# Where the weight slots, h and the feed-forward activations lie in SBUF: new bases, and strides of 8204 and 1028 bytes

## The chip, the cores and the metric

The kernel runs on one core of a Trainium2 chip. The metric is device time in microseconds (us). Three timed runs of the kernel before took 2553.0, 2553.1 and 2554.92 us, a median of 2553.1. A difference of 0.2% (about 5 us) is what such runs can tell from no change.

## The reference

Two transformer stacks run one after the other on one sequence of 256 tokens of width 1024, all in float32. The first has two layers, the second four.

```
for l in range(2):                                     # first stack
    h = rms_norm(x, mix_norm_g[l])
    proj = h @ w_in[l]                                 # 1024 x 2660
    mixed = four mixers (moba, mla, stick-breaking, mamba2) on slices of proj
    x = x + mixed @ w_out[l]
    h = rms_norm(x, ffn_norm_g[l])
    u = causal_dwconv(h @ ffn_w_in[l]) + ffn_conv_b[l]  # 1024 x 5632
    x = x + (silu(gate) * up) @ ffn_w_out[l]            # 2816 x 1024
for i in range(4):                                     # second stack
    x = x + 0.5 * rms_norm(swiglu(rms_norm(x), ff1_w_in[i], ff1_w_out[i]))
    x = x + rms_norm(mixer(rms_norm(x)))               # attention a, gated MLP b, attention c, a
    x = x + 0.5 * rms_norm(swiglu(rms_norm(x), ff2_w_in[i], ff2_w_out[i]))
```

The stick-breaking mixer uses a strict causal mask (key before query, the diagonal left out). Nearly all the arithmetic is in the products with the large weights, about 440 MB of them, each used once.

## The kernel before, in words

The five engines each run their own program (classes Sync, Pool, Scalar, Vector and Tensor), written out by hand in one order and tied by semaphores. Nothing is scheduled by a planner: an engine works its list from top to bottom and waits where the list says so.

Weights stream through the chip in chunks of 1 MB, 128 partitions by 2048 words of 4 bytes. SyncE issues one DMA (or a few) per chunk into a slot of `raw`; there are five slots, and a slot is loaded again when the chunk five places before is done. ScalarE rounds the slot into the slot of the same number of `whi` (the high part, type float32r), VectorE subtracts and writes `wlo` (the low part) in place of `raw`, which shares its memory. A product is then three products: high by high, high by low, and low by high. The activations are split in the same way, into the two halves of `h` (eight blocks of 256 words for the high parts, then eight for the low ones) and, for the inner layer of a feed-forward block, into `hid_hi` and `hid_lo` (22 blocks of 256 words each).

TensorE works through these products in four forms, which the profile names by their lines:

- L734, L735, L736 (`tokens_tile`): the stationary operand is 128 words of a block of `h`, the moving operand 256 words of a weight slot.
- L781, L782, L783 (`features_chunk`): the stationary operand is 128 words of a slot, the moving one 256 words of `h`.
- L798, L799, L801 (`wide_chunk`, the inner layer of the second stack): as the last, but L799 moves the high and the low block of `h` in one matmul of 2 x 256 columns.
- L916 (`block`, the products back to width 1024): the stationary operand is 128 words of `hid_hi`, `hid_lo` or `h`, the moving operand 512 words of a slot.

Every one of these operands is read from SBUF at an address that follows from the base of its tensor, the number of its slot (or block) and the stride between slots (or blocks). The bases follow from the order in which `build` makes the tensors: one behind the other.

At the start, SyncE also issues a DMA for the later part of a table of constants (L549), after the fifth chunk of weights. One of these constants, `strict_add`, is only read once, when VectorE copies it and the identity into `masks` in the type float32r (L2504); TensorE adds the mask in the stick-breaking scores. Both VectorE and TensorE (L1114) wait for the table.

Of the kernel before, what the change touches and what calls it, by code (L numbers as in the profile page):

```python
# [26 lines left out]
F32R = mybir.dt.float32r  # L27
I32 = mybir.dt.int32
# [3 lines left out]
P = 128  # L32
SEQ, D, FF = 256, 1024, 2816
TT = SEQ // P
KT = D // P
FT = FF // P
GROUP, HD = 256, 64
# [3 lines left out]
IN = 3 * GROUP + QR + KVR + ROPE + 3 * GROUP + GROUP + XBC + 4  # L41
# [14 lines left out]
BIG = -1e30  # L56
# [5 lines left out]
SLOTS = 5  # L62
AHEAD = 3
CW = 2048
# [7 lines left out]
CONST = {}  # L72


def constants():

    parts, at = [], 0

    def add(name, a):
        nonlocal at  # L80
        a = np.asarray(a, np.float32)
        parts.append(a)
        CONST[name] = (at, at + a.shape[1])
        at += a.shape[1]

    r, c = np.arange(P)[:, None], np.arange(P)[None, :]
    add("ident", r == c)
    add("minus_half", np.full((P, 16), -0.5))
    for name, dim in (("inv64", HD), ("inv32", ROPE)):
        inv = np.float32(1) / (np.float32(THETA) ** (np.arange(0, dim, 2, dtype=np.float32) / np.float32(dim)))  # L90
        add(name, np.broadcast_to(inv.astype(np.float32), (P, dim // 2)))
    add("upto", r <= c)
    add("ones", np.ones((P, P)))
    add("zeros", np.zeros((P, P)))
    add("causal", np.where(c <= r, 0, BIG))
    add("upto_add", np.where(r <= c, 0, BIG))
    add("strict_add", np.where(r < c, 0, BIG))
    add("from_neg", -(r >= c).astype(np.float32))
    add("ones_neg", -np.ones((P, P)))
    add("dist", -np.abs(np.arange(P)[:, None] + np.arange(SEQ)[None, :] - 127))  # L100
    return np.concatenate(parts, 1)


# [12 lines left out]
ROW_TILES = -(-N_ROWS // P)  # L116
# [389 lines left out]
class Sync(Program):  # L506
# [28 lines left out]
    def mix(self, l):  # L535
        e, m, s, d = self.e, self.m, self.s, self.d
        wv = d.w_in[l].rearrange("(k p) c -> p k c", p=P)

        def pick(raw, j):
            to, of, at = [], [], 0  # L540
            for col, n in IN_PIECES[j][1]:
                to.append(raw[:, :].rearrange("p (k c) -> p k c", k=KT)[:, :, at:at + n])
                of.append(wv[:, :, col:col + n])
                at += n
            return to, of
        for b in range(1 if l == 0 else 0, IN_CHUNKS):
            self.chunk(b, 0, pick)
            if l == 0 and b == 4:
                e.dma_start(m.consts[:, CONST["upto"][0]:], d.consts[:, CONST["upto"][0]:CONST["dist"][0]]).then_inc(s.tables_in, 16)  # L549
        self.advance(IN_CHUNKS)  # L550

    def product_tokens(self, what, l, n):
# [64 lines left out]
class Tensor(Program):  # L617
# [452 lines left out]
    def mix(self, l):  # L1070

        e, m, s = self.e, self.m, self.s
        ps, proj, ident = m.ps, m.proj, m.ident
        r = self.round("mixers")
# [14 lines left out]
        for t in range(TT):  # L1089
            e.transpose(ps[:, 2, t * P:(t + 1) * P], m.cn[:, t, 0:P], ident)  # L1090
            e.transpose(ps[0:64, 2, 256 + t * P:256 + (t + 1) * P], m.cn[:, t, P:QR], ident)
            ins = e.transpose(ps[:, 3, t * P:(t + 1) * P], m.cn[:, t, QR:QR + KVR], ident)
# [18 lines left out]
        chunk(5)  # L1111

        if r == 1:
            e.wait_ge(s.tables_in, 16)  # L1114
        e.wait_ge(s.a_ready, r)
        e.wait_ge(s.up_used, 2 * r)
        for t in range(TT):
# [2 lines left out]
        for t in range(TT):  # L1120
            ins = e.matmul(ps[:, 6, t * 4:t * 4 + 4], m.upto, m.a[:, t, :], start=True, stop=True)
# [753 lines left out]
class Vector(Program):  # L1875
# [582 lines left out]
    def mix(self, l):  # L2458
# [40 lines left out]
        self.split(4, 0)  # L2499
        if l == 0:  # L2500
            self.rotary_angles()
            e.wait_ge(s.tables_in, 16)
            for i, name in enumerate(("ident", "strict_add")):
                ins = e.tensor_copy(m.masks[:, i, :], m.cst(name))  # L2504
            ins.then_inc(s.masks_made, 1)
            self.extend_bias()
        self.split(5, 0)
# [496 lines left out]
def build(nc, d):  # L3004
    with ExitStack() as ctx:
        m = Memory()

        def sb(stack, name, shape, dt=F32):
            return stack.enter_context(nc.sbuf_tensor(name, shape, dt))


        m.whi = sb(ctx, "whi", [P, SLOTS, CW], F32R)
        m.zeros = m.whi[:, SLOTS - 1, 0:256]
        m.x = sb(ctx, "x", [P, TT, D])
        m.xn = sb(ctx, "xn", [P, TT, D])
        m.consts = sb(ctx, "consts", [P, CONST["dist"][0]])
        m.cols = sb(ctx, "cols", [P, ROW_TILES * P])
        m.masks = sb(ctx, "masks", [P, 2, P], F32R)
        m.trig = sb(ctx, "trig", [P, 192])
        m.ss = sb(ctx, "ss", [P, 2])  # L3020
        m.ms = sb(ctx, "ms", [P, 2])
        m.rs = sb(ctx, "rs", [P, 2])
        m.ss2 = sb(ctx, "ss2", [P, 2, 4])
        m.ss3 = sb(ctx, "ss3", [P, 2])
        m.ms2 = sb(ctx, "ms2", [P, 2])
        m.rs2 = sb(ctx, "rs2", [P, 2])
        m.st = sb(ctx, "st", [P, 60])
        m.lam_d = sb(ctx, "lam_d", [P, 4])
        m.ahead = m.lam_d
        m.pos = sb(ctx, "pos", [P, 2])  # L3030
        m.pos_i = sb(ctx, "pos_i", [P, 2], I32)
        m.negmax = sb(ctx, "negmax", [P, 4, 2, 2])
        m.sums = sb(ctx, "sums", [P, 4, 2, 2])
        m.rsum = sb(ctx, "rsum", [P, 4, 6])

        def shared(name, *layouts):

            size, made = 0, []
            for layout in layouts:
                with ExitStack() as inner:  # L3040
                    used = 0
                    for args in layout:
                        made.append(sb(inner, *args))
                        used += int(np.prod(args[1][1:])) * 4
                    size = max(size, used)
            sb(ctx, name, [P, size // 4])
            return made

        (m.rb, m.dt, m.a, m.neg) = shared(
            "mem_scales",  # L3050
            [("rb", [P, SEQ])],
            [("dt", [P, 8, 8]), ("a", [P, TT, 4]), ("neg", [P, 12])])
        (m.raw, m.wlo) = shared(
            "mem_weights",
            [("raw", [P, SLOTS, CW])],
            [("wlo", [P, SLOTS, CW], F32R)])
        m.h = sb(ctx, "h", [P, 2, KT, SEQ], F32R)
        m.h_hi, m.h_lo = m.h[:, 0, :, :], m.h[:, 1, :, :]
        (m.hid_hi, m.hid_lo, m.proj, m.z0, m.z1, m.z2, m.xh, m.xdt, m.bias, m.v, m.qk, m.b_w, m.b_rows, m.b_uv, m.b_wt) = shared(
            "mem_hidden",  # L3060
            [("hid_hi", [P, FT, SEQ], F32R), ("hid_lo", [P, FT, SEQ], F32R)],
            [("proj", [P, TT, IN]), ("z0", [P, 4, 3 * P]), ("z1", [P, 4, 3 * P]), ("z2", [P, 4, 3 * P]), ("xh", [P, TT, GROUP]), ("xdt", [P, TT, GROUP])],
            [("bias", [P, 16, SEQ]), ("v", [P, TT, D]), ("qk", [P, 16, SEQ])],
            [("b_w", [P, 8, P]), ("b_rows", [P, 2, D]), ("b_uv", [P, TT, 2 * D]), ("b_wt", [P, 8, P])])
        (m.u, m.silu, m.hid, m.junk, m.diag, m.prob, m.prob_t, m.prob4, m.rope_tmp, m.moba_x, m.rows) = shared(
            "mem_small",
            [("u", [P, RING, 2, SEQ]), ("silu", [P, RING, SEQ]), ("hid", [P, RING, SEQ])],
# [34 lines left out]
        z1 = m.z1[:, :, :].rearrange("p h c -> p (h c)")  # L3102
        m.ang0, m.turns, m.ang = (z1[:, i * 192:(i + 1) * 192] for i in range(3))
        m.ext = z1[0:32, 576:576 + 3 * P]
        m.y = m.xc[:, 0:2, :]
        m.zs = m.xc[:, 2:4, :]
        m.head_sqs = [m.z1[:, :, :].rearrange("p h c -> p (h c)")[:, i * 512:(i + 1) * 512].rearrange("p (t c) -> p t c", t=TT) for i in range(3)]
# [86 lines left out]
```

## Time and profile before

| | us |
|---|---|
| median of three timed runs | 2553.1 |
| the profiled execution, timed | 2554.75 |
| the span of its instructions | 2552.9 |
| TensorE matmul busy | 2534.4 |
| TensorE weight load busy | 2257.4 |
| VectorE busy | 1770.3 |
| ScalarE busy | 1400.6 |
| GpSimd busy | 156.1 |

The profiled execution took 1.85 us more than its span, and 1.65 us more than the median of the timed runs. A matmul's recorded duration includes its way through the array, so neighbours overlap: a row with a mean of 390 ns does not stand for 390 ns of the span. What a matmul costs in a stream is the distance from its start to the start of the next. It is read from starts in the timeline, or from a count of matmuls in a stretch in which the engine never idles.

### The profile page before, as it was taken

Reading aid. Unit: us, or ns where it says so; the run is one execution under the profiler, and the core shown is the slowest. Engines: PE = TensorE matmul, PEld = TensorE weight load, DVE = VectorE, ACT = ScalarE, POOL = GpSimd, SP = SyncE. Lnnn points to the kernel's source line nnn. Section 1 sums busy time; section 2 is a strip of 40 time slices with the busy share of each in tenths; the row PEclk is TensorE's granted clock in tenths of the full one; section 3 lists DMA queues with packets and bytes.
Section 4 is the critical chain, followed back from the end, with each engine's and each line's share of the span. In section 5 each row is a group of like instructions: output and inputs, shape, how many; then the busy total and the mean of one; then the engine's idle time right before and its main releaser. Section 6 shows DMA issues by size and latency. Waiting matters only on the chain.

```text
span 2552.9 us, 38595 instructions
## 1 busy us (share of the span) xinstructions
PE 2534.4 (99%) x15929; PEld 2257.4 (88%) x15929; DVE 1770.3 (69%) x2517; ACT 1400.6 (55%) x2098; POOL 156.1 (6%) x228
## 2 busy tenths in 40 slices
PE   9999999999999999999999999999999999999998
PEld 8999899998888988888888888888988888898987
DVE  6778567785775677757756775775777567566773
ACT  7756477654554555545555554554655455455652
POOL 2100011000000000000010000002010000010000
PEclk9999999999999999999999999999999999999999
DMA  7267543665765547667665766755467567563863
GB/s 226 94 171 213 179 150 98 176 188 182 192 196 198 190 139 201 196 179 194 197 211 151 205 186 180 202 187 188 155 167 204 185 179 205 185 204 122 217 195 118
DMA packets 568297, 459.96 MB, mean 180 GB/s; under 512 B 10298, under 2 KB 529290, under 8 KB 568122
## 3 DMA queue, kind: packets, MB, share of 16 engines
q1 hardware_dynamic: 562615, 441.91, 58.5%
q0 software_dynamic: 4656, 15.30, 1.7%
q8 instruction: 126, 2.06, 0.3%
q10 hardware_dynamic: 851, 0.28, 0.0%
q14 instruction: 49, 0.40, 0.0%
HBM read 456.37 MB, written 1.10 MB: 179 GB/s over the span
## 4 chain that ended last, share of the span: by engine, by line
PE 94%; DVE 3%; ACT 1%; DMA 1%; issue 0%; POOL 0%; SPq 0%; DVEq 0%; POOLq 0%; ACTq 0%
PE ps L916 28%; PE ps L799 23%; PE ps L798 10%; PE ps L781 5%; PE ps L783 5%; PE ps L782 5%; PE ps L734 4%; PE ps L736 4%; PE ps L735 4%; PE ps L801 1%; PE ps L657 1%; DVE wlo L1890 1%; DMA raw<-in_w_in 1%; PE ps L1017 1%; PE ps L1003 0%; DVE xc L2549 0%
## 5 line engine op out<-in xcount | busy, mean ns | idle before, releaser
L1890 DVE TENSOR_TENSOR wlo<-raw,whi 128x2048 fp32r<-128x2048 f32 (+1 forms) x419 | 956.6, 2286 | 391.0 <-ACT whi L1314 390.8
L1314 ACT ACTIVATE whi<-raw 128x2048 fp32r<-128x2048 f32 (+2 forms) x421 | 800.6, 1907 | 338.1 <-DMA raw<-in_ff_w_out 169.0
L799 PE MATMUL ps<-h,whi 128*128 128x512 f32 x2560 | 865.1, 390 | 0.0
L798 PE MATMUL ps<-h,wlo 128*128 128x256 f32 x2240 | 627.5, 280 | 0.0
L799 PEld LDWEIGHTS ps<-h,whi 128*128 128x128 f32 x2560 | 460.4, 188 | 76.7
L798 PEld LDWEIGHTS ps<-h,wlo 128*128 128x128 f32 x2240 | 420.5, 188 | 13.8
L1314 ACT ACTIVATE u<-ps 128x512 f32<-128x512 f32 x160 | 95.7, 598 | 374.0 <-PE ps L799 373.8
L916 PE MATMUL ps<-whi,hid_lo 128*128 128x512 f32 x880 | 296.1, 396 | 0.0
L916 PE MATMUL ps<-whi,hid_hi 128*128 128x512 f32 x880 | 295.0, 394 | 0.0
L916 PE MATMUL ps<-wlo,hid_hi 128*128 128x512 f32 x880 | 294.4, 394 | 0.0
L781 PE MATMUL ps<-h,whi 128*128 128x256 f32 x1024 | 288.1, 281 | 0.0
L734 PE MATMUL ps<-whi,h 128*128 128x256 f32 (+2 forms) x992 | 283.3, 286 | 3.8 <-ACT proj L1314 2.0
L783 PE MATMUL ps<-h,wlo 128*128 128x256 f32 x1024 | 286.4, 280 | 0.0
L782 PE MATMUL ps<-h,whi 128*128 128x256 f32 x1024 | 286.0, 279 | 0.0
L736 PE MATMUL ps<-whi,h 128*128 128x256 f32 (+2 forms) x992 | 278.4, 281 | 0.0
L735 PE MATMUL ps<-wlo,h 128*128 128x256 f32 (+2 forms) x992 | 278.4, 281 | 0.0
L916 PEld LDWEIGHTS ps<-whi,hid_hi 128*128 128x128 f32 x880 | 165.9, 189 | 38.0
L916 PEld LDWEIGHTS ps<-whi,hid_lo 128*128 128x128 f32 x880 | 165.2, 188 | 38.9
L2251 DVE TENSOR_TENSOR u<-ps,u 128x512 f32<-128x512 f32 x160 | 110.6, 691 | 127.6 <-ACT u L1314 127.3
L916 PEld LDWEIGHTS ps<-wlo,hid_hi 128*128 128x128 f32 x880 | 165.1, 188 | 38.2
L734 PEld LDWEIGHTS ps<-whi,h 128*128 128x128 f32 x992 | 189.0, 191 | 7.8 <-issue 5.0
L781 PEld LDWEIGHTS ps<-h,whi 128*128 128x128 f32 x1024 | 192.6, 188 | 3.0 <-issue 3.0
(321 smaller groups left out, 3203.5 us busy)
## 6 DMA issues: line engine op xcount, KB each, us to landing
raw<-in_ff_w_in SPq DMA_DIRECT2D x176, 1024.0 KB, 6.1
raw<-in_ff_w_out SPq DMA_DIRECT2D x88, 1024.0 KB, 4.9
raw<-in_ffn_w_in SPq DMA_DIRECT2D x44, 1024.0 KB, 6.1
raw<-in_a_w_qkv SPq DMA_DIRECT2D x24, 1024.0 KB, 5.2
raw<-in_ffn_w_out SPq DMA_DIRECT2D x22, 1024.0 KB, 4.9
raw<-in_w_in SPq DMA_DIRECT2D x18, 1024.0 KB, 6.2
raw<-in_c_w_qkv SPq DMA_DIRECT2D x12, 1024.0 KB, 5.3
raw<-in_w_out SPq DMA_DIRECT2D x8, 1024.0 KB, 5.0
```

The costliest lines, as they stand in the source:

```text
L734: e.matmul(out, hi, w_hi, start=(k == 0), stop=False)
L735: e.matmul(out, hi, w_lo, start=False, stop=False)
L736: self.last = e.matmul(out, lo, w_hi, start=False, stop=(k == KT - 1))
L781: e.matmul(out, hi, m.h_hi[:, k, :], start=(k == 0), stop=False)
L782: e.matmul(out, hi, m.h_lo[:, k, :], start=False, stop=False)
L783: ins = e.matmul(out, lo, m.h_hi[:, k, :], start=False, stop=(k == KT - 1))
L798: e.matmul(out[:, 0:SEQ], lo, m.h[:, 0, k, :], start=False, stop=False, skip_group_check=True)
L799: ins = e.matmul(view(out, a=2), hi, m.h[:, :, k, :], start=(k == 0), stop=(k == KT - 1), skip_group_check=True)
L916: self.last = e.matmul(m.ps[:, base + 2 * t + h, :], x, w[:, k, h * 512:(h + 1) * 512], start=(first and k == 0 and n == 0), stop=(last an ...
L1314: return self.nc.scalar.activation(*a, **k)
L1890: self.e.tensor_tensor(chunk_view(m.wlo[:, slot, :], c), chunk_view(m.raw[:, slot, :], c), chunk_view(m.whi[:, slot, :], c).bitcast(F32), ...
L2251: e.tensor_tensor(u, bank[:, :, 0:SEQ], u, ALU.add).then_inc(s.dve_step, 1)
```

## The change

The tensors are made in another order, and three of them get a gap behind each block.

- `masks`, `trig`, `negmax` and `sums` (together 1920 bytes a partition) are made first, so `whi` starts at byte 18432. Behind it come `x`, `xn`, `raw` with `wlo`, `h` and the shared memory of the activations. The small tensors and the constants come after these.
- Slots of `whi`, `raw` and `wlo` are 2051 words long, and 2048 are used: 8204 bytes from slot to slot.
- Blocks of `h`, `hid_hi` and `hid_lo` are 257 words long, and 256 are used: 1028 bytes from block to block.
- To make room, `strict_add` moves to the end of the table of constants and is no longer kept in `consts`. It is loaded by a DMA of its own into `m.strict`, 512 bytes of `z2` (a tensor of the mixers), and read from there once. The two waits for the table count both DMAs.

The starts per partition, as the two programs are built:

| operand | start before | stride before | start now | stride now |
|---|---|---|---|---|
| `whi`, slot | 16512 | 8192 | 18432 | 8204 |
| `raw`, `wlo`, slot | 84896 | 8192 | 75840 | 8204 |
| `h`, block | 125856 | 1024 | 116864 | 1028 |
| `hid_hi`, block | 142240 | 1024 | 133312 | 1028 |
| `hid_lo`, block | 164768 | 1024 | 155936 | 1028 |

Before, each of these starts is a multiple of 32 bytes. Now slot s starts 12 s bytes, and block k starts 4 k bytes, behind a multiple of 16: slots 1, 2 and 3 and three blocks of four are off a multiple of 16 bytes, the others are on one.

```diff
-    add("strict_add", np.where(r < c, 0, BIG))
     add("from_neg", -(r >= c).astype(np.float32))
     add("ones_neg", -np.ones((P, P)))
     add("dist", -np.abs(np.arange(P)[:, None] + np.arange(SEQ)[None, :] - 127))
+    add("strict_add", np.where(r < c, 0, BIG))
...
                 e.dma_start(m.consts[:, CONST["upto"][0]:], d.consts[:, CONST["upto"][0]:CONST["dist"][0]]).then_inc(s.tables_in, 16)
+                e.dma_start(m.strict, d.consts[:, CONST["strict_add"][0]:CONST["strict_add"][1]]).then_inc(s.tables_in, 16)
...
-            e.wait_ge(s.tables_in, 16)
+            e.wait_ge(s.tables_in, 32)
...
-            for i, name in enumerate(("ident", "strict_add")):
-                ins = e.tensor_copy(m.masks[:, i, :], m.cst(name))
+            for i, mask in enumerate((m.ident, m.strict)):
+                ins = e.tensor_copy(m.masks[:, i, :], mask)
...
-        m.whi = sb(ctx, "whi", [P, SLOTS, CW], F32R)
+        m.masks = sb(ctx, "masks", [P, 2, P], F32R)
+        m.trig = sb(ctx, "trig", [P, 192])
+        m.negmax = sb(ctx, "negmax", [P, 4, 2, 2])
+        m.sums = sb(ctx, "sums", [P, 4, 2, 2])
+        m.whi = sb(ctx, "whi", [P, SLOTS, CW + 3], F32R)[:, :, 0:CW]
...
+            [("raw", [P, SLOTS, CW + 3])],
+            [("wlo", [P, SLOTS, CW + 3], F32R)])
+        m.raw, m.wlo = m.raw[:, :, 0:CW], m.wlo[:, :, 0:CW]
+        m.h = sb(ctx, "h", [P, 2, KT, SEQ + 1], F32R)[:, :, :, 0:SEQ]
...
+            [("hid_hi", [P, FT, SEQ + 1], F32R), ("hid_lo", [P, FT, SEQ + 1], F32R)],
...
+        m.hid_hi, m.hid_lo = m.hid_hi[:, :, 0:SEQ], m.hid_lo[:, :, 0:SEQ]
...
+        m.strict = m.z2[:, 0, 0:P]
```

No matmul is added, removed or moved, and none changes its shape. Two places show an instruction more. The first is SyncE's list at the start of the program (`raw` are the slots, `consts` the kept table, `z` the tensor that holds the strict mask for its one use), before:

```order
9 L371 DMA rows<-in_b_b_s 8x128
10 L525 DMA raw<-in_w_in 128x8x224
11 L525 DMA raw<-in_w_in 128x8x4
12 L525 DMA raw<-in_w_in 128x8x256 x3
13 L549 DMA consts<-in_consts 128x1024
14 L525 DMA raw<-in_w_in 128x8x256 x6
15 L525 DMA raw<-in_w_out 128x2x1024 x4
```

and now:

```order
9 L371 DMA rows<-in_b_b_s 8x128
10 L525 DMA raw<-in_w_in 128x8x224
11 L525 DMA raw<-in_w_in 128x8x4
12 L525 DMA raw<-in_w_in 128x8x256 x3
13 L549 DMA consts<-in_consts 128x896
14 L550 DMA z<-in_consts 128x128
15 L525 DMA raw<-in_w_in 128x8x256 x6
16 L525 DMA raw<-in_w_out 128x2x1024 x4
```

The table's DMA has lost 128 of its 1024 columns, and a DMA with these 128 stands behind it, ahead of the sixth chunk of weights. The second place is VectorE's list in the first layer's mixers, before:

```order
35 L1941 TENSOR_SCALAR z<-z 128x192
36 L2504 CAST masks<-consts 128x128 x2
37 L1901 TENSOR_SCALAR z<-consts,z 32x127
38 L1890 TENSOR_TENSOR wlo<-raw,whi 128x2048
39 L2510 TENSOR_REDUCE st<-rope_tmp 128x16
```

and now:

```order
35 L1942 TENSOR_SCALAR z<-z 128x192
36 L2505 CAST masks<-consts 128x128
37 L2505 CAST masks<-z 128x128
38 L1902 TENSOR_SCALAR z<-consts,z 32x127
39 L1891 TENSOR_TENSOR wlo<-raw,whi 128x2048
40 L2511 TENSOR_REDUCE st<-rope_tmp 128x16
```

The two copies stand where they stood; the second reads `z`. Where a copy or a sum writes two neighbouring blocks of `h` at once, its shape is now 128x2x256 in place of 128x512.

## Rows read from the trace of the kernel before

**Rows 1.** The page: busy us (share of the span) x instructions of each engine.

```profile
PE 2534.4 (99%) x15929; PEld 2257.4 (88%) x15929; DVE 1770.3 (69%) x2517; ACT 1400.6 (55%) x2098; POOL 156.1 (6%) x228
```

**Rows 2.** The page: chain that ended last, share of the span by engine, by line.

```profile
PE 94%; DVE 3%; ACT 1%; DMA 1%; issue 0%; POOL 0%; SPq 0%; DVEq 0%; POOLq 0%; ACTq 0%
PE ps L916 28%; PE ps L799 23%; PE ps L798 10%; PE ps L781 5%; PE ps L783 5%; PE ps L782 5%; PE ps L734 4%; PE ps L736 4%; PE ps L735 4%; PE ps L801 1%; PE ps L657 1%; DVE wlo L1890 1%; DMA raw<-in_w_in 1%; PE ps L1017 1%; PE ps L1003 0%; DVE xc L2549 0%
```

**Rows 3.** Waits of TensorE, longest in total: us, times, longest.

```profile
PE ps L734 <- ACT proj L1314: 2.0, 1, 2.0
PE ps L1249 <- DVE z L2634: 1.8, 2, 0.9
...
PE ps L734 <- DVE wlo L1890: 0.6, 1, 0.6
```

**Rows 4.** Groups by line: shapes xcount | busy us, mean ns | idle before.

```profile
L799 PE MATMUL ps<-h,whi 128*128 128x512 f32 x2560 | 865.1, 390 | 0.0
L798 PE MATMUL ps<-h,wlo 128*128 128x256 f32 x2240 | 627.5, 280 | 0.0
L916 PE MATMUL ps<-whi,hid_lo 128*128 128x512 f32 x880 | 296.1, 396 | 0.0
L916 PE MATMUL ps<-whi,hid_hi 128*128 128x512 f32 x880 | 295.0, 394 | 0.0
L916 PE MATMUL ps<-wlo,hid_hi 128*128 128x512 f32 x880 | 294.4, 394 | 0.0
...
L736 PE MATMUL ps<-whi,h 128*128 128x256 f32 x928 | 260.8, 281 | 0.0
L735 PE MATMUL ps<-wlo,h 128*128 128x256 f32 x928 | 260.8, 281 | 0.0
```

**Rows 5.** Timeline of TensorE: start us, us, instruction; a stretch of the wide form.

```profile
1030.02 0.28 PE L798 MATMUL ps<-h,wlo 128*128 128x256 f32 x1
1030.14 0.39 PE L799 MATMUL ps<-h,whi 128*128 128x512 f32 x1
1030.37 0.28 PE L798 MATMUL ps<-h,wlo 128*128 128x256 f32 x1
...
1031.40 0.28 PE L798 MATMUL ps<-h,wlo 128*128 128x256 f32 x1
```

**Rows 6.** Windows: stretch and length, busy (count) by engine, PEclk, DMA share, GB/s.

```profile
1080.00:1120.00 40.00, 40.00 (x174) 32.40 (x173) 16.74 (x8) 13.87 (x10) 0.00 (x0) 1.00 0.58 184
165.00:255.00 90.00, 90.00 (x771) 90.00 (x770) 78.45 (x122) 57.37 (x84) 6.46 (x12) 1.00 0.73 202
10.00:40.00 30.00, 27.31 (x222) 26.73 (x223) 20.41 (x36) 22.66 (x34) 10.84 (x19) 0.96 1.06 327
1130.00:1175.00 45.00, 45.00 (x297) 41.04 (x296) 33.83 (x45) 27.38 (x39) 3.26 (x6) 1.00 0.84 219
```

**Rows 7.** VectorE lines that read at shifting word offsets: ns min/median/max, first and last start.

```profile
L2547 DVE TENSOR_SCALAR xc<-xt,cols x8: 403/404/408, 68.6 to 386.1; 128x256 f32<-128x256 f32 x8
L2549 DVE SCALAR_TENSOR_TENSOR xc<-xt,cols,xc x24: 475/479/489, 70.0 to 391.2; 128x256 f32<-128x256 f32 x24
```

**Rows 8.** The chain's pieces at the start of the program: start us, us, what.

```profile
22.48 0.13 PE ps L736
22.62 11.15 DMA raw<-in_w_in
33.80 1.91 ACT whi L1314
```

**Rows 9.** Timeline of SyncE at the start: start us, us, instruction, count.

```profile
13.15 2.92 SPq L549 DMA_DIRECT2D consts<-in_consts  x1
16.11 39.90 SPq L525 DMA_DIRECT2D raw<-in_w_in  x6
```

**Rows 10.** VectorE's copies into the masks: ns min/median/max, first and last start us.

```profile
L2504 DVE CAST masks<-consts x2: 220/220/221, 46.5 to 46.6; 128x128 fp32r<-128x128 f32 x2
```

More of the change, by code:

```diff
@@ L2501, in mix @@
             self.rotary_angles()
-            e.wait_ge(s.tables_in, 16)
-            for i, name in enumerate(("ident", "strict_add")):
-                ins = e.tensor_copy(m.masks[:, i, :], m.cst(name))
+            e.wait_ge(s.tables_in, 32)
+            for i, mask in enumerate((m.ident, m.strict)):
+                ins = e.tensor_copy(m.masks[:, i, :], mask)
             ins.then_inc(s.masks_made, 1)
@@ L3015, in build, with shared @@
         m.xn = sb(ctx, "xn", [P, TT, D])
+        def shared(name, *layouts):
+            size, made = 0, []
+            for layout in layouts:
+                with ExitStack() as inner:
+                    used = 0
+                    for args in layout:
+                        made.append(sb(inner, *args))
+                        used += int(np.prod(args[1][1:])) * 4
+                    size = max(size, used)
+            sb(ctx, name, [P, size // 4])
+            return made
+        (m.raw, m.wlo) = shared(
+            "mem_weights",
+            [("raw", [P, SLOTS, CW + 3])],
+            [("wlo", [P, SLOTS, CW + 3], F32R)])
+        m.raw, m.wlo = m.raw[:, :, 0:CW], m.wlo[:, :, 0:CW]
+        m.h = sb(ctx, "h", [P, 2, KT, SEQ + 1], F32R)[:, :, :, 0:SEQ]
+        m.h_hi, m.h_lo = m.h[:, 0, :, :], m.h[:, 1, :, :]
+        (m.hid_hi, m.hid_lo, m.proj, m.z0, m.z1, m.z2, m.xh, m.xdt, m.bias, m.v, m.qk, m.b_w, m.b_rows, m.b_uv, m.b_wt) = shared(
+            "mem_hidden",
+            [("hid_hi", [P, FT, SEQ + 1], F32R), ("hid_lo", [P, FT, SEQ + 1], F32R)],
+            [("proj", [P, TT, IN]), ("z0", [P, 4, 3 * P]), ("z1", [P, 4, 3 * P]), ("z2", [P, 4, 3 * P]), ("xh", [P, TT, GROUP]), ("xdt", [P, TT, GROUP])],
+            [("bias", [P, 16, SEQ]), ("v", [P, TT, D]), ("qk", [P, 16, SEQ])],
+            [("b_w", [P, 8, P]), ("b_rows", [P, 2, D]), ("b_uv", [P, TT, 2 * D]), ("b_wt", [P, 8, P])])
         m.consts = sb(ctx, "consts", [P, CONST["dist"][0]])
         m.cols = sb(ctx, "cols", [P, ROW_TILES * P])
-        m.masks = sb(ctx, "masks", [P, 2, P], F32R)
-        m.trig = sb(ctx, "trig", [P, 192])
         m.ss = sb(ctx, "ss", [P, 2])
@@ L3031, in build @@
         m.pos_i = sb(ctx, "pos_i", [P, 2], I32)
-        m.negmax = sb(ctx, "negmax", [P, 4, 2, 2])
-        m.sums = sb(ctx, "sums", [P, 4, 2, 2])
         m.rsum = sb(ctx, "rsum", [P, 4, 6])
[L3036 to L3047, printed above, removed]
         (m.rb, m.dt, m.a, m.neg) = shared(
@@ L3052, in build @@
             [("dt", [P, 8, 8]), ("a", [P, TT, 4]), ("neg", [P, 12])])
[L3053 to L3064, printed above, removed]
+        m.hid_hi, m.hid_lo = m.hid_hi[:, :, 0:SEQ], m.hid_lo[:, :, 0:SEQ]
         (m.u, m.silu, m.hid, m.junk, m.diag, m.prob, m.prob_t, m.prob4, m.rope_tmp, m.moba_x, m.rows) = shared(
```

## The prediction

> **What bounds the kernel now.** I read the busy times first, then the chain, TensorE's waits, the matmul groups, and last windows and a timeline for the cost of one matmul. TensorE's matmuls are busy for 2534.4 of 2552.9 us [rows 1], and the chain of work that ended last runs over TensorE for 94% of the span, nearly all of it in the four forms of the big products [rows 2]. So TensorE waits for almost nothing: 2552.9 - 2534.4 leaves 18.5 us, and its longest single wait is 2.0 us [rows 3]. VectorE at 69% and ScalarE at 55% [rows 1] stand on the chain with 4% together [rows 2], at the edges between stages.
>
> A change of layout can therefore show in three places: in what one matmul costs, in the edges, and in the transfers, if they grow until TensorE waits for them.
>
> What one matmul costs is read from starts. In the wide form an L798 starts at 1030.02 and again at 1030.37 and, four rounds after the first, at 1031.40 [rows 5]: 1.38 us for four rounds, 345 ns for a 256-column matmul and a 512-column one, about 117 and 228. In the products back, 174 matmuls of 512 columns fill 40 us [rows 6]: about 231 ns each. In the first stack's inner layer 771 of 256 columns fill 90 us [rows 6]: 116.7 ns. The clock is granted in full there, at its upper level of 2.4 GHz, so a column a cycle would be 213.3 and 106.7 ns. Each matmul pays 10 to 18 ns more than its columns.
>
> **The change part by part.**
>
> *The operands' addresses.* None of some 14,400 big matmuls (about 5,800 of 512 columns and 8,600 of 256 or a little fewer) goes away or changes its shape. One nanosecond on each would be 14 us, so the answer hangs on a fraction of a nanosecond. Does a matmul's cost follow its operands' addresses? In L735 the moving operand starts at an odd multiple of 32 bytes (`wlo`, 84896), in L736 at an even one (`whi`, 16512), and both have a mean of 281 ns. In L916 the three kinds of product have 394, 394 and 396 ns, and the two with 394 differ in the slot's base, while the 396 has the same moving operand as one of them [rows 4]. So a move by 32 bytes costs 0 to 2 ns and shows no sign. Moves by a word do not occur on TensorE before: every start is a multiple of 32. The nearest rows for those are VectorE's. The taps of the convolution read `xt`, whose rows are 1036 bytes apart, at one, two and three words' offset. The 8 and 24 instructions lie within 403 to 408 and 475 to 489 ns [rows 7], 1% and 3% from end to end for all offsets.
>
> The bounds. Below: were the whole excess over a column a cycle a matter of addresses, and were it to go, 5,800 x 16 + 8,600 x 10 = 179 us would go with it. Above: I take it that a stream is read in groups of words, four to a group; a stream that starts off a multiple of 16 bytes then reads one group more. From 256 to 512 columns the mean goes from 280 to 394 ns [rows 4], 0.445 ns a column, so four columns are 1.8 ns. By the table of starts, 11,700 moving streams are off such a multiple (an L799 has two streams): 21 us. The weight load next to the 256-column matmuls is on the same footing; in 165 to 255 us it is busy all the time [rows 6], so it may pace them, and 5,700 of these loads start off a multiple: 10 us more. I take 0, since the rows nearest, L735 against L736 and VectorE's taps, show no cost of a start; the ends are -179 and +31.
>
> The Trainium skill, "SBUF — State Buffer", section "Specifications (TRN2)", speaks against the change: SBUF has lines of 16 bytes, an access needs at least two hits in a line for full bandwidth, and each crossing to a new line pays a penalty. A stream that starts or ends with a single word in a line would pay by that rule; VectorE's taps above pay at most a few ns, and no row here shows TensorE at such a start. By the rule the sum would go up, by the bound above; by the rows it stays.
>
> *The writers.* ScalarE, VectorE and the edges write `h`, `hid` and the slots at the new starts, and the pairs of blocks as 2x256. By the taps [rows 7] that is 0. Were each of VectorE's and ScalarE's instructions on the chain 1% longer, 4% of 2552.9 is 102 us, so +1 us is the end above. Away from the edges the cover is their idle time, 31% and 45% of the span [rows 1].
>
> *The slots' transfers.* A packet now lands at a start that is no multiple of 32 bytes; no row shows what that costs. The cover is large: in the products back the share of the DMA engines is 0.58, in the first stack's inner layer 0.73, in the densest stretch that I show 0.84, with TensorE never idle [rows 6]. Packets could take 1/0.73 = 1.37 times as long before the inner layer waits. I take 0 there. In 10 to 40 us there is no cover: the share is 1.06 [rows 6], and the chain runs through one transfer that begins when a slot comes free at 22.62 us and lands at 33.80, 11.15 us on [rows 8]. A packet 3% longer is 0.3 us there.
>
> *The mask's own DMA.* It carries bytes that the table's DMA no longer carries, and stands ahead of the six DMAs that SyncE issues from 16.11 us [rows 9]. The first of them for which the chain waits is held until 22.62 us by a slot, not by SyncE, so an issue of under half a microsecond before it has room. Its small packets go through a full queue: up to 0.2 us on the chain. The copies that wait for it start at 46.5 us [rows 10], more than 30 us after the table's issue at 13.15, while a transfer in that full queue takes 11 us [rows 8, 9]. Behind VectorE's wait stand the next `wlo` and the mixers, behind TensorE's the sums; neither waits longer. 0.
>
> *Sum.* The profiled execution took 2554.75 us, span 2552.9 and 1.85 around it. To it come 0.3 + 0.2 = 0.5 at the start and 0 elsewhere: 2555.25. The median of the timed runs stands 1.65 below that execution: 2553.6 us, +0.02%. About 0.2%, 5 us, is what a measurement of this kernel can tell from no change.
>
> **The rivals.**
>
> *Slower by the groups (0.31).* Every stream that starts off a multiple of 16 bytes reads a group more, in TensorE. For it: the cost per column shows no slack in which a fetch could hide, since a 512-column matmul costs 0.445 ns for each added column and not 0.417. Against it: VectorE's taps, and L735 beside L736. The rule of lines on the page "SBUF — State Buffer" of the Trainium skill would have this outcome. It begins to count from 0.4 ns a stream (11,700 x 0.4 = 5 us). Its price is 21 us, 2574.6; with the weight loads 2585.
>
> *Slower by far (0.06).* A word-aligned start is served at a lower rate throughout, by TensorE or by the DMA engines. Were packets to take twice as long, the share of 0.73 in 165 to 255 us [rows 6] would become 1.46, so these 90 us would become 131; with the second layer's that is 82 us, 2636 before the second stack is counted. Nothing in the rows speaks for it but that they can't exclude it.
>
> *Faster by a gentler meeting of the streams (0.23).* The excess of 10 to 18 ns comes from the moving stream and the weight load meeting in SBUF at starts that agree in their low bits, and shifted starts undo a part of it. For it: the excess is there in every form and I have no other cause. Against it: it is the same for both bases [rows 4], and the starts of the two streams drift against each other anyhow. The Trainium skill, "TensorE: Matmul & The Clock Gate", section "Step-by-step: what each phase is for", says that TensorE has two independent read ports, one for each of the streams; no run here shows the ports. A tenth of the 179 us is 18: 2536; a quarter is 45: 2509.
>
> *It doesn't do what it says.* The starts in the table are of the built program, so this is left out.
>
> **How the numbers follow.** No change 0.40, at 2553.6, from 2549 to 2558. Slower by the groups 0.31, some of it (0.03) too small to be told from no change. Slower by far 0.06. Faster 0.23, likewise with 0.02 too small. So faster 0.21, within 0.2% 0.45, slower 0.34. The range reaches over the groups' price with the weight loads, 2590, and to the tenth of the excess, 2535; the quarter and the far case are left out, under 2 in 10. The likeliest case's own range is 2549 to 2558.
>
> **What would show it.** Right: L799, L798 and L916 keep their means of 390, 280 and 394 to 396 ns within 1 ns; TensorE's waits stay those of [rows 3]; the share of the transfers in 165 to 255 us stays near 0.73. Slower by the groups: means 1 to 4 ns up, most in L799, whose two streams both start off, and least in L801, whose block 0 starts on a multiple. Slower by far: TensorE waits for `wlo`, with a DMA behind it, or means up by tens of ns. Faster: means down in all forms. What would make the forecast wrong is a cost or a gain of 0.4 ns a matmul, which no row before can show.

## The result, and the profile after

The changed kernel took 2582.3 us, the median of four runs (2582.17 to 2582.45), against 2553.23 us for the kernel before: a ratio of 1.0112, 95% interval 1.010 to 1.0125. That is 29 us slower, where the likeliest case said no change (2553.6) and the rival "slower by the groups" said 2574.6, or 2585 with the weight loads. Behind the changed lines the line numbers are one higher: L799 is now L800, L916 is L917.

First the page of the changed kernel, busy time by engine (us, share of the span, instructions):

```profile
span 2580.4 us, 38596 instructions
PE 2562.4 (99%) x15929; PEld 2273.2 (88%) x15929; DVE 1771.7 (69%) x2517; ACT 1399.9 (54%) x2098; POOL 158.1 (6%) x228
```

Against [rows 1], matmuls are busy for 28.0 us more, and the span is 27.5 us longer. VectorE, ScalarE and GpSimd moved by 1 to 2 us. The loss is TensorE's own work, then, and no wait. The waits of TensorE say the same (us, times, longest):

```profile
PE ps L1250 <- DVE z L2635: 1.6, 2, 0.8
...
PE ps L735 <- ACT proj L1315: 0.8, 1, 0.8
```

The longest wait of [rows 3], 2.0 us for `proj`, is down to 0.8, and none has come in its place. The groups of matmuls tell where the time went (shapes xcount | busy us, mean ns | idle before):

```profile
L800 PE MATMUL ps<-h,whi 128*128 128x512 f32 x2560 | 883.1, 397 | 0.0
L799 PE MATMUL ps<-h,wlo 128*128 128x256 f32 x2240 | 629.6, 281 | 0.0
L917 PE MATMUL ps<-whi,hid_hi 128*128 128x512 f32 x880 | 296.3, 396 | 0.0
L917 PE MATMUL ps<-whi,hid_lo 128*128 128x512 f32 x880 | 295.3, 394 | 0.0
L917 PE MATMUL ps<-wlo,hid_hi 128*128 128x512 f32 x880 | 295.0, 394 | 0.0
L782 PE MATMUL ps<-h,whi 128*128 128x256 f32 x1024 | 290.5, 284 | 0.0
L783 PE MATMUL ps<-h,whi 128*128 128x256 f32 x1024 | 288.6, 282 | 0.0
L784 PE MATMUL ps<-h,wlo 128*128 128x256 f32 x1024 | 288.1, 281 | 0.0
...
L737 PE MATMUL ps<-whi,h 128*128 128x256 f32 x928 | 261.9, 282 | 0.0
L736 PE MATMUL ps<-wlo,h 128*128 128x256 f32 x928 | 261.7, 282 | 0.0
```

and the same three lines of the first stack's inner layer in the kernel before, which [rows 4] doesn't hold:

```profile
L781 PE MATMUL ps<-h,whi 128*128 128x256 f32 x1024 | 288.1, 281 | 0.0
L783 PE MATMUL ps<-h,wlo 128*128 128x256 f32 x1024 | 286.4, 280 | 0.0
L782 PE MATMUL ps<-h,whi 128*128 128x256 f32 x1024 | 286.0, 279 | 0.0
```

By busy time, L800 lost 883.1 - 865.1 = 18.0 us, L799 2.1, the three of the first stack's inner layer 6.7, the three products of L917 with `hid` only 1.1, and L736 with L737 2.0. That is 29.9 us. At the start 1.4 us come back (below); the rest is in small groups. Counted from start to start, as a matmul's cost is, the sums are much the same: the wide form (L799, L800 and L802) lost 18.9 us, the first stack's inner layer 5.9, L735 to L737 3.2, L917 on `hid` 1.0. Against the kernel before, then, the 512-column matmul that moves two blocks of `h` carries 60% of the loss, and the equally wide one of L917, whose slots moved in the same way, carries next to none. Against the same bases without gaps it looks otherwise (first experiment).

The stretches that the prediction spoke of (length, busy and count by engine, granted clock, DMA share, GB/s):

```profile
1080.00:1120.00 40.00, 40.00 (x174) 32.37 (x173) 19.45 (x11) 16.25 (x11) 0.00 (x0) 1.00 0.55 188
165.00:255.00 90.00, 90.00 (x758) 90.00 (x757) 76.74 (x118) 57.00 (x82) 6.49 (x12) 1.00 0.73 199
10.00:40.00 30.00, 28.59 (x242) 28.08 (x242) 20.39 (x36) 22.56 (x33) 12.97 (x19) 1.00 1.04 326
```

Against [rows 6], the products back make 174 matmuls in 40 us as before, the inner layer 758 in 90 us and not 771 (118.7 ns each, where it was 116.7), and the transfers' share there is still 0.73. The start is not slower: the share is 1.04, and the granted clock is 1.00 where it was 0.96. The chain there (start us, us, what):

```profile
22.04 0.12 PE ps L737
22.18 10.21 DMA raw<-in_w_in
32.41 1.92 ACT whi L1315
```

The transfer starts 0.4 us earlier than in [rows 8] and takes 0.9 us less, so ScalarE begins 1.4 us earlier. In this execution neither the starts of the slots nor the mask's own DMA shows as a cost.

### The profile page after: what moved, and what is told of

Same layout as the page of the kernel before. It is cut to its first block, busy times and chain, and to the rows that moved or that the text cites. A ratio compares the mean times of both kernels' runs of the same rounds, so it can differ in the third digit from the quotient of the medians.

```text
span 2580.4 us, 38596 instructions
## 1 busy us (share of the span) xinstructions
PE 2562.4 (99%) x15929; PEld 2273.2 (88%) x15929; DVE 1771.7 (69%) x2517; ACT 1399.9 (54%) x2098; POOL 158.1 (6%) x228
## 3 DMA queue, kind: packets, MB, share of 16 engines
q1 hardware_dynamic: 562759, 441.91, 58.1%
## 4 chain that ended last, share of the span: by engine, by line
PE 94%; DVE 3%; ACT 1%; DMA 1%; issue 0%; POOL 0%; SPq 0%; DVEq 0%; POOLq 0%; ACTq 0%
PE ps L917 27%; PE ps L800 23%; PE ps L799 10%; PE ps L782 5%; PE ps L783 5%; PE ps L784 5%; PE ps L735 4%; PE ps L736 4%; PE ps L737 4%; PE ps L802 1%; PE ps L658 1%; DVE wlo L1891 1%; DMA raw<-in_w_in 1%; PE ps L1018 0%; PE ps L1004 0%; DVE xc L2550 0%
## 5 line engine op out<-in xcount | busy, mean ns | idle before, releaser
L800 PE MATMUL ps<-h,whi 128*128 128x512 f32 x2560 | 883.1, 397 | 0.0
L799 PE MATMUL ps<-h,wlo 128*128 128x256 f32 x2240 | 629.6, 281 | 0.0
L800 PEld LDWEIGHTS ps<-h,whi 128*128 128x128 f32 x2560 | 460.8, 188 | 89.6
L799 PEld LDWEIGHTS ps<-h,wlo 128*128 128x128 f32 x2240 | 423.5, 189 | 13.6
L917 PE MATMUL ps<-whi,hid_hi 128*128 128x512 f32 x880 | 296.3, 396 | 0.0
L917 PE MATMUL ps<-whi,hid_lo 128*128 128x512 f32 x880 | 295.3, 394 | 0.0
L917 PE MATMUL ps<-wlo,hid_hi 128*128 128x512 f32 x880 | 295.0, 394 | 0.0
L735 PE MATMUL ps<-whi,h 128*128 128x256 f32 (+2 forms) x992 | 283.5, 286 | 2.4 <-DVE h L1953 1.0
L737 PE MATMUL ps<-whi,h 128*128 128x256 f32 (+2 forms) x992 | 279.4, 282 | 0.0
L736 PE MATMUL ps<-wlo,h 128*128 128x256 f32 (+2 forms) x992 | 279.3, 282 | 0.0
L917 PEld LDWEIGHTS ps<-whi,hid_lo 128*128 128x128 f32 x880 | 165.9, 189 | 38.5
L917 PEld LDWEIGHTS ps<-wlo,hid_hi 128*128 128x128 f32 x880 | 165.9, 189 | 38.4
L917 PEld LDWEIGHTS ps<-whi,hid_hi 128*128 128x128 f32 x880 | 165.8, 189 | 37.9
L782 PEld LDWEIGHTS ps<-h,whi 128*128 128x128 f32 x1024 | 193.5, 189 | 3.0 <-issue 3.0
L783 PEld LDWEIGHTS ps<-h,whi 128*128 128x128 f32 x1024 | 194.1, 190 | 0.0
```

The costliest lines, as they stand in the source:

```text
L735: e.matmul(out, hi, w_hi, start=(k == 0), stop=False)
L736: e.matmul(out, hi, w_lo, start=False, stop=False)
L737: self.last = e.matmul(out, lo, w_hi, start=False, stop=(k == KT - 1))
L782: e.matmul(out, hi, m.h_hi[:, k, :], start=(k == 0), stop=False)
L783: e.matmul(out, hi, m.h_lo[:, k, :], start=False, stop=False)
L799: e.matmul(out[:, 0:SEQ], lo, m.h[:, 0, k, :], start=False, stop=False, skip_group_check=True)
```

## The experiments

All times are medians, and ratios are to the kernel before on the same chip with a 95% interval. The runs were on several chips, where the kernel before had medians of 2553.2 to 2553.4 us. "Offset" below is an operand's start within 64 bytes. In the kernel before, `whi` has offset 0, and `wlo`, `h` and `hid` have 32, in every slot and block.

### New bases without gaps

```diff
-        m.whi = sb(ctx, "whi", [P, SLOTS, CW + 3], F32R)[:, :, 0:CW]
+        m.whi = sb(ctx, "whi", [P, SLOTS, CW], F32R)[:, :, 0:CW]
-        m.h = sb(ctx, "h", [P, 2, KT, SEQ + 1], F32R)[:, :, :, 0:SEQ]
+        m.h = sb(ctx, "h", [P, 2, KT, SEQ], F32R)
```

(the same for `raw`, `wlo`, `hid_hi`, `hid_lo`; the order of the tensors and the mask's DMA stay changed; every base is now a multiple of 2048 bytes, and every block of `h` and `hid` starts on a multiple of 1024.)

> The new order of the tensors and the mask's own DMA, with slots 8192 and blocks 1024 bytes apart, so every operand starts on a multiple of 32 bytes again, and whi, h and hid on a multiple of 2048. Theory A (a moving stream that starts off a multiple of 16 bytes costs): as before, 2553 within 3 us, L800 back at a mean of 390 ns. Rival B (it is the new bases or their distances, not the odd starts): it keeps most of the 29 us, above 2570. Rival C (round bases are better and the gaps take more than 29 us back): under 2545.

2556.8 us, 1.0014 (1.0006 to 1.0023): most of the loss hangs on the gaps. But the bases are not free. The groups, as above:

```profile
L800 PE MATMUL ps<-h,whi 128*128 128x512 f32 x2560 | 876.1, 396 | 0.0
L799 PE MATMUL ps<-h,wlo 128*128 128x256 f32 x2240 | 624.6, 279 | 0.0
...
L917 PE MATMUL ps<-whi,hid_hi 128*128 128x512 f32 x880 | 291.3, 390 | 0.0
L917 PE MATMUL ps<-whi,hid_lo 128*128 128x512 f32 x880 | 290.5, 389 | 0.0
L917 PE MATMUL ps<-wlo,hid_hi 128*128 128x512 f32 x880 | 290.5, 389 | 0.0
```

L800's busy time rose by 11.0 us against [rows 4] (6 ns in its mean), and the three products with `hid` fell by 4 to 7 (-13.2 us in all). From start to start, the first stack's inner layer takes 8.2 us more as well. Effects of starts that are all multiples of 32 cancel almost to nothing.

This kernel differs from the changed one by the gaps alone. Against it, from start to start, the changed kernel loses 15.0 us in L917 on `hid` and 3.9 on `h`, 9.4 in the wide form, and wins back 2.3 in the first stack's inner layer. Which form seems to pay depends on the layout that one compares with.

### Gaps in h alone

```diff
-        m.h = sb(ctx, "h", [P, 2, KT, SEQ], F32R)
+        m.h = sb(ctx, "h", [P, 2, KT, SEQ + 1], F32R)[:, :, :, 0:SEQ]
```

(from the kernel without gaps; `hid_hi` and `hid_lo` keep blocks of 1024 bytes.)

> As round_only, and the blocks of h 1028 bytes apart, slots and hid without gaps. Theory A: nearly all of the loss, since L800 (means up by 7 ns on 2560 matmuls, 18 us) and L782 to L784 (up 2 ns on 3072, 5 us) move h: 2574 to 2579, and L917 and L735 to L737 as in round_only. A rival that puts the cost on the weight slots (odd writes and packets, or odd stationary operands in L800): under 2560.

2580.0 us, 1.0101 (1.0085 to 1.0116): 23 us over the kernel without gaps, from `h` alone.

```profile
L800 PE MATMUL ps<-h,whi 128*128 128x512 f32 x2560 | 882.8, 397 | 0.0
...
L917 PE MATMUL ps<-whi,hid_hi 128*128 128x512 f32 x880 | 296.7, 396 | 0.0
L917 PE MATMUL ps<-wlo,hid_hi 128*128 128x512 f32 x880 | 296.0, 395 | 0.0
L917 PE MATMUL ps<-whi,hid_lo 128*128 128x512 f32 x880 | 295.9, 395 | 0.0
```

L917 on `hid` lost 16 us, though within 64 bytes all its operands stand at the same offsets as in the kernel without gaps. The timelines of the two show it. First the kernel without gaps (start us, us, instruction, two to a row; two rows are left out in each):

```profile
1080.40 0.62 PE L917 MATMUL ps<-whi,hid_hi 128*128 128x512 f32 x2
...
1081.76 0.62 PE L917 MATMUL ps<-whi,hid_hi 128*128 128x512 f32 x2
```

and then the one with gaps in `h`:

```profile
1079.69 0.63 PE L917 MATMUL ps<-whi,hid_hi 128*128 128x512 f32 x2
...
1081.09 0.63 PE L917 MATMUL ps<-whi,hid_hi 128*128 128x512 f32 x2
```

Six matmuls take 1.36 us in the one (227 ns each) and 1.40 in the other (233). Both run at that pace, without a wait, through the whole of each such stage. At the granted clock, 1.00 of 2.4 GHz, that is 544 and 560 cycles for 512 columns.

Two things differ for L917 here. The stage before it has other operands, and behind the longer `h` the tensors of `hid` stand 64 bytes further from the slots. No run moves `hid` by 64 bytes against the slots and leaves the stage before as it was, so these 6 ns can't be put down to one of the two. That the offsets alone don't set a pace shows within the kernel before. Near the end of the products back its L916 takes the same products in the same order in all ten of its stages on `hid`, and the stage of the first layer and the second one of the second stack begin with the same slot too, so every operand stands at the same address. Behind the first layer's inner layer it looks so:

```profile
313.67 0.40 PE L916 MATMUL ps<-wlo,hid_hi 128*128 128x512 f32 x1
...
325.58 0.39 PE L916 MATMUL ps<-wlo,hid_hi 128*128 128x512 f32 x1
```

and in that stage of the second stack so:

```profile
1113.24 0.39 PE L916 MATMUL ps<-wlo,hid_hi 128*128 128x512 f32 x1
...
1125.03 0.39 PE L916 MATMUL ps<-wlo,hid_hi 128*128 128x512 f32 x1
```

From the first row to the last are 51 matmuls, in 11.91 us (233.5 ns each) and in 11.79 (231.2). Both stages of the first stack end at the one pace and all eight of the second at the other. So a stream can settle in more than one pace on the same operands. What is seen to differ here is the form of the inner layer before it.

### Gaps in the slots alone

```diff
-        m.whi = sb(ctx, "whi", [P, SLOTS, CW], F32R)[:, :, 0:CW]
+        m.whi = sb(ctx, "whi", [P, SLOTS, CW + 3], F32R)[:, :, 0:CW]
```

(from the kernel without gaps; `raw` and `wlo` likewise.)

> As round_only, and the slots of whi, raw and wlo 8204 bytes apart, h and hid without gaps. Theory A: the matmuls that move a slot alone pay, L735 to L737 1 to 2 ns and L917 0 to 1: 2555 to 2560; L800 at 390 although its stationary operand starts off a multiple of 16 bytes in three slots of five. The rival that puts the cost on the slots: above 2570.

2567.78 us, 1.0057 (1.0045 to 1.007). L800 is at 394 ns, L917 at 395 to 396. With the gaps in `h` (+23) this +11 would make 34; the changed kernel, with both and those of `hid`, has +25.5. The costs don't add. L917 on `hid` is slow again, and here too `hid` stands elsewhere against the slots: 128 bytes further from `whi`, 64 from `wlo`.

### Gaps of 16 bytes

```diff
-        m.whi = sb(ctx, "whi", [P, SLOTS, CW + 3], F32R)[:, :, 0:CW]
+        m.whi = sb(ctx, "whi", [P, SLOTS, CW + 4], F32R)[:, :, 0:CW]
-        m.h = sb(ctx, "h", [P, 2, KT, SEQ + 1], F32R)[:, :, :, 0:SEQ]
+        m.h = sb(ctx, "h", [P, 2, KT, SEQ + 4], F32R)[:, :, :, 0:SEQ]
```

(from the changed kernel; `raw` and `wlo` as `whi`; `hid` has blocks of 1024 bytes. Every start is a multiple of 16.)

> As round_only, with gaps of four words: slots 8208 and blocks of h 1040 bytes apart (hid without gaps), so that the strides are off the powers of two and every start is on a multiple of 16 bytes. Theory A: as round_only within 3 us. The rival that puts the cost on strides off the powers of two, or on the distance of the high from the low block: 2570 or more.

2569.03 us, 1.0056 (1.0044 to 1.0069), 12 us over the kernel without gaps. So starts off a multiple of 16 are not the whole of it: no stream has one here. L800 is at 395 ns, L917 again at 394 to 395. Three things can be behind the 12 us, and the run doesn't separate them: the steps of 16 bytes within 64, the strides themselves, and the base of `raw` and `wlo`, which the longer slots put 32 bytes past a multiple of 64.

### Everything 64 bytes on

```diff
+        sb(ctx, "gap", [P, 16])
         m.whi = sb(ctx, "whi", [P, SLOTS, CW], F32R)[:, :, 0:CW]
```

(from the kernel without gaps.)

> As round_only (no gaps), with 64 bytes before whi, so that whi, wlo, h and hid all start 64 bytes past a multiple of 2048 and their distances stay. Theory D (a matmul's cost follows the distance of the moving stream from the stationary operand): as round_only, L917 on hid near 389 ns, L800 near 396, 2557. Theory F (it follows where the operand itself starts within a round block of 512 or 2048 bytes): L917 on hid back at 394 to 396, 2568 or more.

2560.0 us, 1.0028 (1.0017 to 1.0039). The means of L800, L799 and L917 are those of the kernel without gaps (396, 279, and 390, 389, 389). The profiled execution, 2564.71 us and the longest of the seven, waits 3.4 us for `proj` at the start, at a granted clock of 0.96 in the first 40 us, which also lifts the mean of L735 to L737 by 1 ns; what makes the medians differ by 3.2 us is not shown.

The transfers do tell the two apart. SyncE's queue (packets, MB, share of 16 engines' time), first in the kernel without gaps, then here:

```profile
q1 hardware_dynamic: 562759, 441.91, 55.0%
```

```profile
q1 hardware_dynamic: 562759, 441.91, 57.9%
```

The six kernels here whose slots of `raw` start at multiples of 2048 bytes lie at 54.5 to 55.0%; the eight others, among them the one before and the changed one, at 57.8 to 58.5%. TensorE's means don't follow it.

### h and hid 256 and 512 bytes on

```diff
+        m.consts = sb(ctx, "consts", [P, CONST["dist"][0]])
         m.h = sb(ctx, "h", [P, 2, KT, SEQ], F32R)
...
-        m.consts = sb(ctx, "consts", [P, CONST["dist"][0]])
```

(from the kernel without gaps; this is the 256. For the 512 it is the tensor `cols` that is made ahead of `h`.)

> As round_only, with h and hid 256 bytes past a multiple of 2048 and whi and wlo on one. Theory F with a block of 256: L917 on hid stays at 389; with a block of 512 or more: 394. Theory D: 394. L800, L782 to L784 move h now 256 bytes past: by F as in round_only if the block is 256.

> As round_only, with h and hid 512 bytes past a multiple of 2048 and whi and wlo on one. Theory F with a block of 512: L917 on hid stays at 389 ns and L800 at 396, 2557. Theory D: L917 goes to 393 or more.

2557.03 us, 1.0018 (1.0008 to 1.0027), and 2558.53 us, 1.0019 (1.001 to 1.0029). The means are once more those of the kernel without gaps, but for 1 ns in L735 to L737 at the start. So four layouts give one set of means: for TensorE nothing changed when all bases moved on by 64 bytes together, or `h` and `hid` by 256 or 512 against the slots. A shift of 64 or 128 bytes against the slots was not tried by itself.

### h and hid 32 bytes on

```diff
+        sb(ctx, "gap", [P, 8])
         m.h = sb(ctx, "h", [P, 2, KT, SEQ], F32R)
```

> As round_only, with 32 bytes before h, so that h and hid start 32 bytes past a multiple of 2048 and whi and wlo on one. Theory D: L917 on hid goes to 394, as in h_only, where hid stood 64 bytes off. Theory F: the same. For L800 theory F says no better than 396 as its stationary operand stays; theory D lets it move either way by up to 6 ns. If 32 bytes change nothing (L917 389), only 64 bytes and up count.

2561.28 us, 1.0034 (1.0019 to 1.0048). Here the means move: L800 393 in place of 396, L917 396, 395 and 396 in place of 390, 389 and 389. An offset of 32 bytes counts, with either sign.

### h alone 32 bytes on

(as the last, with another 32 bytes ahead of `hid`, which so is back at offset 0.)

```diff
+        sb(ctx, "gap", [P, 8])
         m.h = sb(ctx, "h", [P, 2, KT, SEQ], F32R)
+        sb(ctx, "gap2", [P, 8])
```

> As h_32, with 32 bytes more before hid, so that hid is back on a multiple of 64 and only h stands 32 bytes past one. Theory H: L800 at 393 and L782 to L784 at 280 as in h_32, and L917 on hid at 389 as in round_only: some 15 us under h_32, about 2546. If a pattern once entered is kept (as L917 did in h_only, whose hid, whi and wlo stood as in round_only within 64 bytes), L917 stays at 395: 2561.

2562.3 us, 1.0037 (1.0024 to 1.005). L917 on `hid` stays at 395 to 396 ns, with its operands at the offsets within 64 bytes that gave 389. As with the gaps in `h`, the stage before differs, and `hid` stands 64 bytes further from the slots; the run doesn't tell which decided.

### wlo and h 32 bytes on, hid at 0

```diff
+        sb(ctx, "gap", [P, 8])
         (m.raw, m.wlo) = shared(
...
+        sb(ctx, "gap2", [P, 8])
         (m.hid_hi, m.hid_lo, m.proj, ...
```

(offsets as in the kernel before, except for `hid`, at 0 in place of 32.)

> Within 64 bytes whi at 0, wlo and h at 32, as in the kernel before, and hid at 0, where before it is at 32. Theory H: L800 at 390 and L799 at 280 as before; L917 on hid between 389 and 395, since wlo and hid now differ by 32: 2538 to 2553, the best so far if the lower end holds.

2553.68 us, 1.0001 (0.9991 to 1.001).

```profile
L800 PE MATMUL ps<-h,whi 128*128 128x512 f32 x2560 | 865.2, 390 | 0.0
L799 PE MATMUL ps<-h,wlo 128*128 128x256 f32 x2240 | 627.5, 280 | 0.0
```

These are the rows of the kernel before [rows 4] to 0.1 us, at other bases. The version with `h` alone 32 bytes on differs from this one by the place of `raw` and `wlo` alone, and there L800 took 393: the offset of `wlo`, an operand of its neighbour L799, is part of what L800 costs. The 389 ns of L917 did not come with it, so this version gains nothing over the kernel before.

### Everything 4 bytes on, everything 16 bytes on

```diff
-        m.h = sb(ctx, "h", [P, 2, KT, SEQ], F32R)
+        m.h = sb(ctx, "h", [P, 2 * KT * SEQ + 16], F32R)[:, 1:2 * KT * SEQ + 1].rearrange("p (a k c) -> p a k c", a=2, k=KT)
```

(from the kernel without gaps; `whi`, `raw`, `wlo`, `hid_hi` and `hid_lo` likewise. For the 16 bytes the 1 is a 4, in all of them.)

> As round_only (no gaps), with every operand of the big matmuls 4 bytes on: all slots and blocks start one word past a multiple of 64. Theory A (a stream that starts off a multiple of 16 bytes reads a group more): L800, L917 and the 256-column matmuls 1.8 ns or more above round_only, L917 on hid 391 or more, 2580 or more. Theory H (what counts is how the starts of moving and stationary operands stand to one another within 64 bytes, and a common shift is free): as round_only, 2557, L800 396 ns, L917 on hid 389.

> round_only with every operand of TensorE (whi, wlo, h, hid_hi, hid_lo) 16 bytes on, no gaps: all starts are 16 behind a multiple of 64, so the offsets between any two operands are those of round_only and of all_4 (which stood 4 bytes on and took 2612.4 us). Theory 'off a multiple of 16': a start costs when it cuts a line of 16 bytes; all starts here are multiples of 16, so the time is round_only's, 2557 us (2554 to 2561), the means are its 396, 280 and 389 ns within 1 ns, and the 56 us of all_4 were the odd word. Theory 'place within 64 bytes': a stream that doesn't start on a multiple of 64 reads one stretch of 64 bytes more, whatever the multiple of 16; the means of the products back go up as in all_4, by about 10 ns, and the time is 2590 to 2612 us. In between, 2561 to 2590, both count.

2612.38 us, 1.0229 (1.0214 to 1.0244), and 2564.65 us, 1.0045 (1.0028 to 1.0062). The groups of the first:

```profile
L800 PE MATMUL ps<-h,whi 128*128 128x512 f32 x2560 | 890.1, 399 | 0.0
L799 PE MATMUL ps<-h,wlo 128*128 128x256 f32 x2240 | 631.5, 282 | 0.0
L917 PE MATMUL ps<-whi,hid_lo 128*128 128x512 f32 x880 | 299.9, 400 | 0.0
L917 PE MATMUL ps<-wlo,hid_hi 128*128 128x512 f32 x880 | 299.0, 398 | 0.0
L917 PE MATMUL ps<-whi,hid_hi 128*128 128x512 f32 x880 | 298.9, 399 | 0.0
```

and of the second:

```profile
L800 PE MATMUL ps<-h,whi 128*128 128x512 f32 x2560 | 876.9, 395 | 0.0
L799 PE MATMUL ps<-h,wlo 128*128 128x256 f32 x2240 | 629.3, 281 | 0.0
L917 PE MATMUL ps<-wlo,hid_hi 128*128 128x512 f32 x880 | 295.7, 395 | 0.0
L917 PE MATMUL ps<-whi,hid_lo 128*128 128x512 f32 x880 | 294.7, 394 | 0.0
L917 PE MATMUL ps<-whi,hid_hi 128*128 128x512 f32 x880 | 291.0, 389 | 0.0
```

Between these two only the common shift differs. At 4 bytes in place of 16 the mean of every big form is higher, L800 by 4 ns, L917 by 3 to 10, and the whole takes 47.7 us more. Against the kernel without gaps the 16 bytes cost 7.9 us, but there the shift is not all: the spare words behind the tensors also put `wlo`, `h`, `hid_hi` and `hid_lo` 64, 128, 192 and 256 bytes further from `whi`. The theory that only what cuts a multiple of 16 counts expected 2557 us and the other 2590 to 2612; the time lies near the first, so most of the 55.6 us of the first version goes with the start off a multiple of 16, and something else counts too.

## Why the prediction was right and wrong

The range, 2535 to 2590, holds the 2582.3 us because it was drawn over the price of a rival that had 0.31. The likeliest case, no change at 2549 to 2558, did not come about.

*What bounds the kernel: right.* TensorE's matmuls took the whole change, 28.0 us for a span 27.5 us longer, and the granted clock was at its upper level, 1.00 of 2.4 GHz, in all stretches shown.

*The writers, the transfers, the mask's DMA: right, within 2 us.* The costliest line of VectorE, which reads and writes at the new starts, after (shapes xcount | busy us, mean ns | idle before):

```profile
L1891 DVE TENSOR_TENSOR wlo<-raw,whi 128x2048 fp32r<-128x2048 f32 x416 | 951.8, 2291 | 382.6 <-ACT whi L1315 382.4
```

and before:

```profile
L1890 DVE TENSOR_TENSOR wlo<-raw,whi 128x2048 fp32r<-128x2048 f32 x416 | 951.2, 2290 | 385.8 <-ACT whi L1314 385.6
```

It takes 1 ns longer. At the start the sum put +0.5 us, and it came out at -1.4. The mask's own DMA held SyncE for 0.80 us, more than the half microsecond that the step allowed, and the slot's release at 22 us covers it (start us, us, instruction):

```profile
12.53 2.87 SPq L549 DMA_DIRECT2D consts<-in_consts  x1
15.44 0.80 SPq L550 DMA_DIRECT2D z<-in_consts  x1
16.29 37.23 SPq L525 DMA_DIRECT2D raw<-in_w_in  x6
```

*The operands' addresses: this step failed.* "I take 0, since the rows nearest, L735 against L736 and VectorE's taps, show no cost of a start." Measured it is about +30 us, at the bound above (+31). There are two faults in the inference. VectorE's taps say nothing of TensorE, whose 512-column matmuls pay 3 to 10 ns for starts off a multiple of 16, between the runs with everything 4 and 16 bytes on. And L735 with L736, neighbours in one stream, were read as two measurements of an address. A matmul's cost includes its neighbours' operands, as the 3 ns of L800 for the place of `wlo` show, so that L735 and L736 both have 281 ns excludes nothing. The rows of L916, from which the step read that 32 bytes are worth 0 to 2 ns, fell by 4 to 7 ns in the kernel without gaps, where the offset of `wlo` and `hid` went from 32 to 0.

*The rival "slower by the groups": its sign came out, its mechanism in part, its place and its size by luck.* It priced 21 to 31 us. It said that most would be lost in L799 (now L800) and least in L801 (now L802). Against the kernel before that came out, though L800 lost 7 ns and not 4 at most. Against the same bases without gaps it did not: L800 lost 1 ns, L802 3 (a mean of 277.5, then 280.6), and L917 on `hid` 5 to 6. The pair of runs at 4 and 16 bytes is its cleanest test, though at one pair of offsets, and starts off a multiple of 16 do cost: 47.7 us over some 14,400 big matmuls, about 3.3 ns each with all operands off. It had 1.8 ns per moving stream; 47.7 us over 14,400 + 2,560 such streams are 2.8, if the weight loads have no part in it. The Trainium skill, "SBUF — State Buffer", section "Specifications (TRN2)", speaks of 16-byte lines and a price for each crossing, and these two runs agree with its sign. But the version with gaps of 16 bytes, which by this mechanism are free, took 12 us more. From the kernel before to the changed one the steps are +3.6 us (the bases), +12.2 (gaps of 16 bytes) and +13.3 (gaps of 12 and 4 in their place, and those of `hid`). The second has no start off a multiple of 16 in it; the third is the only one that the rival's mechanism can claim, and it isn't a pure one, since the offsets in steps of 16 change with it. That the total fell near the price is luck.

*"Faster by a gentler meeting of the streams": such a gain exists in one form, the whole went the other way, and the meeting of the streams is not shown.* New bases without gaps took L917 from 394 to 396 down to 389 to 390 ns, so a part of the excess over 213.3 ns is to be had back: start to start 227 in place of about 232. No layout tried had that together with the 390 ns of L800.

What stays open: why the paces lie where they do, and whether the 6 ns of L917 hang on the stage before or on 64 bytes between `hid` and the slots. The runs show that the operands' starts, the neighbour's among them, set the pace, and that in the kernel before something besides the starts does, by 2 ns. No run separates the fetch of the weights from that of the moving operand, or either from what the other engines write meanwhile.

## What to carry to other kernels

Where a kernel is bound by a stream of matmuls, treat the operands' starts as a tuning parameter: keep them at multiples of 16 bytes at the least (4 bytes cost 47.7 us over 16 here), and measure every change of bases by group, since a gain in one form and a loss in another can cancel in the total. Rows of one steady stream that agree with each other don't show that an address is free: only a run with another address does. And a price known from one engine is no evidence for another.

## What the runs showed of the hardware

- 512-column matmuls with a full granted clock ran back to back, with no wait recorded, at 227 ns or at 233 ns for whole stages, with the same offsets within 64 bytes. In the kernel before, the same products from the same addresses ran at 233 ns at the end of a stage in the first stack and at 231 in the second.
- Everything 64 bytes on, or `h` and `hid` 256 or 512 bytes on, left the means of L800, L799 and L917 as they were; `h` and `hid` 32 bytes on moved those of L800 and L917 by 3 to 7 ns, down and up.
- All operands 4 bytes on cost 55.6 us of 2556.8; 16 bytes on, 7.9 us. In both the tensors also stand up to 256 bytes further apart.
- Transfers into slots that start off a multiple of 32 bytes took no more than in the kernel before, whose slots start 32 bytes past a multiple of 64: a DMA share of 0.73 in both in the inner layer, and 58.1% of the engines' time over the span for SyncE's queue, where it was 58.5%. Into slots at multiples of 2048 bytes they took 55%.
